# Cache pages laid out in 32 partitions with four tokens each, in place of 128 partitions with one

## The chip, the cores and the metric

One core of a Trainium2 chip runs the whole program in one launch. The metric is device microseconds from start to end, the median of the runs shown. All arithmetic is fp32, with matmul operands split into a high and a low part.

## The reference

One inference step of one decoder layer for two groups that share the weights: a prompt of 256 tokens, and 8 sample sequences of one new token each, whose past of 1024 tokens lies in paged caches (8 pages of 128 tokens for each sequence, found through `page_table`). The layer is: half a SwiGLU feed-forward, one input projection, two attention branches, an output projection, another half feed-forward.

For the samples, branch A (8 heads of 64) takes the scores of the new query against 1024 past keys, sums the keys in blocks of 256 tokens, keeps the three past blocks whose mean scores highest, adds ALiBi and does a softmax over these and the new token. Branch B (4 heads, two score maps of 64 each, values of 128) attends to all past tokens and subtracts lambda times the second softmax from the first. Each of the four caches (keys and values, A and B) holds rows of 512 numbers, 2 KB for each token, so a page is 256 KB in one piece of memory. All 8 sequences with 8 pages in four caches come to 256 pages, 64 MB.

What matters for the change: a softmax with ALiBi and block sums can take the tokens in any order, if the distance of each token and the block to which it belongs are known.

## The kernel before

The program is written out engine by engine, with semaphores between them; the order of each engine and of each DMA queue is the order in its block of code. The stages are: feed-forward 1, projection (w_in), the key stage (about 393 to 542 us), softmax beside the last two gate blocks (542 to 560 us), the value stage with the prompt's own attention (560 to 660 us), branch and output projections, feed-forward 2.

**Slots.** `kv` has two buffers for each of the branches A and B, and `kv_lent` one more, so `KVS` is 3. A buffer is [128, 4, 512], 8 KB in each partition, and holds half a sequence: four pages. One filling is called a use: uses 0 to 15 are keys, 16 to 31 are values, and each use brings 4 pages for A and 4 for B, 2 MB together. `load_half` (L380) issues four DMAs of one page; page q goes to column q of all 128 partitions, one token of 2 KB in each. A's are issued by SyncE, B's by GpSimd, from `kv_load`, which first waits until the use three before has been consumed, and for each new sequence reads 8 page numbers into registers (`page_ids`, L373). SyncE's queue also carries the 1 MB weight blocks (`load_w`, L448), one for each sequence in the key stage.

**Key stage.** `chunk_turn` (L1396) transposes for each chunk of 128 features the four pages' tokens into a PSUM bank, ScalarE (A, L716) and VectorE (B, L414) copy it to SBUF, and `chunk_scores` (L1405) multiplies by the padded query. Half a gate block (L1186 to L1188) stands behind each use of the first six sequences. The scores of all sequences and heads gather in two banks: partition = (head, sequence), column = token, 128 a page.

**Softmax.** VectorE reduces the scores to 4 block sums (L1036), ranks them (L1042 to L1048), adds page offset and penalty into 8 scalars (L1050), and writes `prob` = score + scalar + distance row for each page (L1052); ScalarE does the exponent; TensorE turns `prob` by a permutation (L1448).

**Value stage.** For each sequence and half, four matmuls with A's pages and four with B's (L1477): weights `wpad` (token = partition, page = column) against the page. Between them stand the prompt's scores, transposes and products. A slot comes free through `s_pv` when its four matmuls have ended, and `kv_load` then waits for it. After the last: the sample outputs are extracted (L1514) and the branch projections begin.

Of the kernel before, what the change touches and what calls it, by code (L numbers as in the profile page):

```python
# [19 lines left out]
ALU = mybir.AluOpType  # L20
ACT = mybir.ActivationFunctionType
AX = mybir.AxisListType

P = 128
# [9 lines left out]
PAST = 1024  # L34
# [8 lines left out]
KVS = 3  # L43
# [60 lines left out]
def _columns():  # L104
    at = 0
    for name, w in (("ident", 128), ("blockdiag", 128), ("ones", 128), ("half", 2), ("sel9", 9), ("sel8", 8), ("perm", 128), ("sel4", 4),
                    ("negslope", 1), ("pageslope", 8), ("coef1", 1), ("coeflam", 1), ("rowA", 1), ("tri", 16),
                    ("dist", 384), ("distrow", 128), ("maskA", 512), ("maskB", 512)):
        CW[name] = (at, w)
        at += w  # L110
    return at

NCONST = _columns()

def slope_of_row(j):

    return 2.0 ** -(j + 1) if j < 8 else 2.0 ** (-2.0 * ((j - 8) // 2 + 1))

def constants():
    c = np.zeros((P, NCONST), np.float32)

    def put(name, a):
        c[:, CW[name][0]:CW[name][0] + CW[name][1]] = a

    p = np.arange(P)
    put("ident", np.eye(P))
    put("blockdiag", p[:, None] // 64 == p[None] // 64)  # L130
    put("ones", 1.0)
    put("half", np.stack([p < 64, p >= 64], 1))
    put("sel9", (p[:, None] % 32) == np.arange(9)[None])

    row_s, row_j = p % 32 // 4, 8 * (p % 4 // 2) + 2 * (p // 32) + p % 2
    put("sel8", row_s[:, None] == np.arange(8)[None])

    put("perm", (64 * (row_j // 8) + 8 * row_s + row_j % 8)[:, None] == p[None])

    put("sel4", (p[:, None] % 32 // 8) == np.arange(4)[None])  # L140
    slope = np.array([slope_of_row(j) for j in row_j])
    put("negslope", -slope[:, None])
    put("pageslope", slope[:, None] * 128.0 * np.arange(8)[None])
    isb1 = (row_j >= 8) & (p % 2 == 1)
    put("coef1", (~isb1)[:, None])
    put("coeflam", isb1[:, None])
    put("rowA", (row_j < 8)[:, None])
    n = np.arange(4)
    put("tri", np.broadcast_to((n[None, :] < n[:, None]).reshape(1, 16), (P, 16)))
    k = np.arange(256)  # L150
    d0 = np.where(k[None, :128] <= p[:, None], p[:, None] - k[None, :128], BIG)
    d1 = np.where(k[None] <= p[:, None] + 128, p[:, None] + 128 - k[None], BIG)
    put("dist", np.concatenate([d0, d1], 1))
    put("distrow", np.broadcast_to(PAST - np.arange(128)[None], (P, 128)))
    col = np.arange(512)
    put("maskA", col[None] // 64 == p[:, None] % 8)
    put("maskB", col[None] // 128 == p[:, None] % 8 // 2)
    return c
# [26 lines left out]
def build(nc, A, O):  # L185
    ctx = ExitStack()
    with ctx:
# [3 lines left out]
        def place(name, shape, dt=F32, where=None):  # L191
            size = int(np.prod(shape[1:])) * 4
            where = where if where is not None else at
            h = nc.alloc_sbuf_tensor_at(name, shape, dt, offset=where[0])
            where[0] = (where[0] + size + 31) // 32 * 32
            assert where[0] <= end, (name, where[0], end)
            return h

        def sem(name):
            return ctx.enter_context(nc.semaphore(name))  # L200
# [7 lines left out]
        x = place("x", [P, KC, T])  # L208
# [15 lines left out]
        r = [region]  # L224
# [7 lines left out]
        r = [region]  # L232
# [5 lines left out]
        r = [region]  # L238
# [8 lines left out]
        stat = place("stat", [P, 64], where=r)  # L247
# [5 lines left out]
        r = [area]  # L253
# [4 lines left out]
        r = [area]  # L258
        kTs = [[place(f"kTs{a}{s}", [P, 512], where=r) for s in range(2)] for a in "AB"]
        r = [area]  # L260
        prob = place("prob", [P, PAST], where=r)
        b0 = place("b0", [P, P], where=r)
        ecur = place("ecur", [P, P], where=r)
        dcur = place("dcur", [TS, P], where=r)
        plog = [place(f"plog{h}", [P, 384], where=r) for h in range(2)]
        pts_at = r[0]
        r = [area]
        om = place("om", [P, 2, 512], where=r)
        r = [pts_at]
# [6 lines left out]
        r = [hlo_at]  # L276
        wpad = [place(f"wpad{s}", [P, NPG, 2, 56], where=r) for s in range(2)]

        bank = ctx.enter_context(nc.psum_tensor("bank", [P, 8, 512], F32))

        def C(name, lo=0, hi=None):
            a, w = CW[name]
            return const[:, a + lo:a + (w if hi is None else hi)]
# [22 lines left out]
        s_kv = [[sem(f"kv_landed{a}{s}") for s in range(KVS)] for a in "AB"]  # L306
# [59 lines left out]
        def kv_slot(ab, use):  # L366
            if use % KVS < KVS - 1:
                return kv[ab][use % KVS]
            return kv_lent[ab]

        def page_ids(eng, s):

            _, ids = nc.values_load_multi_w_load_instructions(A["page_table"][s:s + 1, 0:NPG], engines=[eng.engine], min_val=0, max_val=NPHYS - 1)  # L373
            return ids

        def load_half(eng, ab, cache, ids, half, use):

            for q in range(4):
                page = ids[4 * half + q]
                eng.dma_start(kv_slot(ab, use)[:, q, :], cache[bass.ds(page, 1)].rearrange("a t d -> (a t) d")).then_inc(s_kv[ab][use % KVS], 16)  # L380

        def kv_landed(use):
            return 64 * (use // KVS + 1)
# [3 lines left out]
        def kv_load(eng, ab, use):  # L387

            s, half = divmod(use % 16, 2)
            if half == 0:  # L390
                held[ab] = page_ids(eng, s)
            prev = use - KVS
            if use == KVS - 1:
                if ab == 0:
                    eng.wait_ge(s_lo, half_done(LENT_LAST, 1))
                else:
                    eng.wait_ge(s_ecur, 1)
            if 0 <= prev < 16:
                eng.wait_ge(s_kTs[ab], 4 * prev + 4)
            elif prev >= 16:  # L400
                eng.wait_ge(s_pv, 2 * (prev - 16) + ab + 1)
            load_half(eng, ab, (CACHE_K if use < 16 else CACHE_V)[ab], held[ab], half, use)
# [405 lines left out]
        def _(v):  # L808
            ch = Chain(v, s_vch)
            dve = nc.vector  # L810
# [222 lines left out]
            v.wait_ge(s_const_late, 16)  # L1033
            ch.link(dve.tensor_scalar(b0[:, :], C("distrow"), C("negslope"), None, ALU.mult))
            blk = stat[:, 8:12]
            ch.link(dve.tensor_reduce(blk, bank[:, 6:8, :].rearrange("p a (b n) -> p (a b) n", n=256), AX.X, ALU.add))  # L1036

            bm = blk.unsqueeze(1).broadcast_to([P, 4, 4])
            bn = blk.unsqueeze(2).broadcast_to([P, 4, 4])
# [6 lines left out]
            ch.link(dve.tensor_reduce(stat[:, 12:16], gt, AX.X, ALU.add))  # L1046
            ch.link(dve.tensor_scalar(stat[:, 12:16], stat[:, 12:16], 2.5, -BIG, ALU.is_gt, ALU.mult))
            ch.link(dve.tensor_scalar(stat[:, 12:16], stat[:, 12:16], C("rowA"), None, ALU.mult))  # L1048
            pen = stat[:, 12:16].unsqueeze(2).broadcast_to([P, 4, 2])
            ch.link(dve.tensor_tensor(stat[:, 48:56].rearrange("p (b g) -> p b g", b=4), C("pageslope").rearrange("p (b g) -> p b g", b=4), pen, ALU.add))  # L1050
            for g in range(NPG):
                ins = dve.scalar_tensor_tensor(out=prob[:, 128 * g:128 * g + 128], in0=bank[:, 6 + g // 4, 128 * (g % 4):128 * (g % 4) + 128],  # L1052
                                               scalar=stat[:, 48 + g:49 + g], in1=b0[:, :], op0=ALU.add, op1=ALU.add)
            ch.link(ins)
            ch.link(dve.tensor_reduce(stat[:, 2:3], prob[:, :], AX.X, ALU.max))
            ch.link(dve.tensor_tensor(stat[:, 2:3], stat[:, 2:3], ncur[:, :], ALU.max))
# [34 lines left out]
            for c in range(KC):  # L1091
                for h in range(2):
                    j = 2 * c + h
# [43 lines left out]
            for q in range(4):  # L1137
                ab, half = q // 2, q % 2
# [8 lines left out]
                g = gT[:, 8 * ab + 4 * half:8 * ab + 4 * half + 4, :]  # L1147
# [441 lines left out]
```

## Time and profile before

| what | value |
|---|---|
| median of 3 runs | 937.45 us (935.45 to 940.9) |
| profiled execution | 942.06 us, of which the span from first to last instruction is 940.4 |
| TensorE busy, weight loads busy | 834.4 us, 709.4 us |
| VectorE, ScalarE, GpSimd busy | 459.4, 359.0, 80.3 us |
| mean granted TensorE clock | 0.941 |
| moved by DMA | 209.73 MB, mean 223 GB/s |

TensorE is busy for 89% of the span, but the share is a mean over stages. The second part of the page cuts the span into 40 slices of 23.5 us; the digits are tenths. The chain of waits names what ended last at each moment. "DMA share" is the mean busy share of 16 DMA engines. `kvA` and `kvB` are the two own buffers of each branch, `kvA_lent` and `kvB_lent` the third.

### The profile page before, as it was taken

To read this page: it belongs to the slowest core of one execution; us is meant where nothing else is said; L and a number is where in the kernel's file an instruction comes from. 1 tells how busy PE (TensorE), PEld (TensorE's weight loads), DVE (VectorE), ACT (ScalarE), POOL (GpSimd) and SP (SyncE) were. 2 spreads that over 40 slices of the span, in tenths; PEclk is the share of its full clock that TensorE was granted. 3 is DMA by queue.
4 is the path that set the end of the run, shared out by engine and by line. 5 is a ranking of instruction groups with operands and counts; after the bars stand their busy time and mean duration, and the time that the engine had idled before them with its cause. 6 is when DMAs were issued, how large, how long until landed. Compare 5 with 4: busy or idle time off the path is not lost.

```text
span 940.4 us, 16984 instructions
## 1 busy us (share of the span) xinstructions
PE 834.4 (89%) x6366; PEld 709.4 (75%) x6366; DVE 459.4 (49%) x674; ACT 359.0 (38%) x539; POOL 80.3 (9%) x150
## 2 busy tenths in 40 slices
PE   3789999999997999689989896776989799999997
PEld 1369898989996989667767471321789699999997
DVE  1344444435436768634343364543475655555442
ACT  1344433343335454433233333321343544444341
POOL 0000000000001010222121213131000000000000
PEclk9789999999998999999999997787689799999999
DMA  8679898886766763578878858988045155555540
GB/s 317 239 253 307 275 310 267 295 294 196 257 230 233 249 205 106 181 246 276 282 244 287 311 176 298 345 318 308 1 135 179 48 181 181 180 191 172 178 147 24
DMA packets 146232, 209.73 MB, mean 223 GB/s; under 512 B 6693, under 2 KB 100148, under 8 KB 146172
## 3 DMA queue, kind: packets, MB, share of 16 engines
q1 hardware_dynamic: 134336, 170.97, 54.9%
q0 software_dynamic: 11360, 36.80, 11.0%
q10 hardware_dynamic: 476, 1.17, 0.3%
q8 instruction: 36, 0.59, 0.2%
q14 instruction: 24, 0.20, 0.1%
HBM read 205.67 MB, written 3.24 MB: 222 GB/s over the span
## 4 chain that ended last, share of the span: by engine, by line
PE 74%; DVE 7%; issue 6%; DMA 5%; ACT 4%; SPq 2%; POOLq 1%; POOL 0%; ACTq 0%; DVEq 0%
PE bank L1186 19%; PE bank L1187 18%; PE bank L1188 17%; PE bank L1396 6%; PE bank L1405 4%; PE bank L1213 4%; DVE rstd L967 2%; SPq L373 1%; ACT kTsA L716 1%; PE bank L1222 1%; DMA crow<-in_c_rows 1%; PE bank L1229 1%; DMA kvA_lent<-in_cache_v_moba 1%; PE bank L1477 1%; DMA raw<-in_w_ada 1%
## 5 line engine op out<-in xcount | busy, mean ns | idle before, releaser
L818 DVE TENSOR_TENSOR wlo<-raw,whi 128x1024 fp32r<-128x1024 f32 (+1 forms) x192 | 227.3, 1199 | 241.4 <-ACT whi L571 239.3
L1186 PE MATMUL bank<-hhi,whi 128*128 128x264 f32 x1088 | 321.8, 296 | 15.4 <-DVE hlo L858 12.9
L1187 PE MATMUL bank<-hlo,whi 128*128 128x264 f32 x1088 | 313.1, 288 | 0.0
L1188 PE MATMUL bank<-hhi,wlo 128*128 128x264 f32 x1088 | 312.5, 287 | 0.0
L571 ACT ACTIVATE whi<-raw 128x1024 fp32r<-128x1024 f32 (+1 forms) x192 | 194.8, 1036 | 134.2 <-PE bank L1188 79.5
L1186 PEld LDWEIGHTS bank<-hhi,whi 128*128 128x128 f32 x1088 | 209.1, 192 | 40.0 <-issue 29.5
L1187 PEld LDWEIGHTS bank<-hlo,whi 128*128 128x128 f32 x1088 | 210.2, 193 | 0.2
L1188 PEld LDWEIGHTS bank<-hhi,wlo 128*128 128x128 f32 x1088 | 208.8, 192 | 0.0
L1186 PE MATMUL bank<-ahi,whi 128*128 128x264 f32 x416 | 121.2, 291 | 4.0 <-DVE alo L1158 4.0
L1188 PE MATMUL bank<-ahi,wlo 128*128 128x264 f32 x416 | 119.2, 286 | 0.0
L1187 PE MATMUL bank<-alo,whi 128*128 128x264 f32 x416 | 119.1, 286 | 0.0
L1186 PEld LDWEIGHTS bank<-ahi,whi 128*128 128x128 f32 x416 | 79.5, 191 | 5.3 <-issue 5.0
L414 DVE COPY kTsB<-bank 128x512 f32<-128x512 f32 x64 | 41.8, 686 | 81.2 <-PE bank L1405 76.8
L1187 PEld LDWEIGHTS bank<-alo,whi 128*128 128x128 f32 x416 | 79.5, 191 | 0.2
L1188 PEld LDWEIGHTS bank<-ahi,wlo 128*128 128x128 f32 x416 | 79.6, 191 | 0.0
L716 ACT ACTIVATE kTsA<-bank 128x512 f32<-128x512 f32 x64 | 34.8, 595 | 86.6 <-PE bank L1405 81.5
L380 POOL DMA_DIRECT2D kvB<-in_cache_k_diff x44 | 23.6, 537 | 300.5 <-issue 235.7
L600 ACT ACTIVATE sil<-bank 128x528 f32<-128x528 f32 x22 | 13.4, 611 | 78.1 <-PE bank L1188 78.1
L1213 PE MATMUL bank<-raw,csilu 128*32 128x512 f32 x288 | 39.0, 660 | 2.4 <-DMA raw<-in_w_ada 2.1
L1396 PE MATMUL bank<-const,kvA 128*128 128x128 f32 x176 | 27.3, 279 | 13.2 <-ACT kTsA L716 13.2
L1396 PEld LDWEIGHTS bank<-const,kvA 128*128 128x128 f32 x176 | 20.3, 143 | 24.4 <-issue 21.1
L1405 PE MATMUL bank<-kTsA,qpad 128*32 128x512 f32 x128 | 34.7, 611 | 0.8 <-ACT kTsA L716 0.8
(215 smaller groups left out, 773.0 us busy)
## 6 DMA issues: line engine op xcount, KB each, us to landing
raw<-in_w_ada SPq DMA_DIRECT2D x36, 1024.0 KB, 7.4
raw<-in_ffn_w_gate SPq DMA_DIRECT2D x22, 1024.0 KB, 5.4
raw<-in_ffn_w_up SPq DMA_DIRECT2D x22, 1024.0 KB, 5.8
raw<-in_w_in SPq DMA_DIRECT2D x20, 1024.0 KB, 7.3
raw<-in_ffn_w_down SPq DMA_DIRECT2D x16, 1024.0 KB, 5.3
kvB<-in_cache_k_diff POOLq DMA_DIRECT2D x44, 256.0 KB, 5.8
kvA<-in_cache_k_moba SPq DMA_DIRECT2D x44, 256.0 KB, 4.1
kvA<-in_cache_v_moba SPq DMA_DIRECT2D x44, 256.0 KB, 5.9
```

The source lines that it names most:

```text
L380: eng.dma_start(kv_slot(ab, use)[:, q, :], cache[bass.ds(page, 1)].rearrange("a t d -> (a t) d")).then_inc(s_kv[ab][use % KVS], 16)
L414: copy(kTs[ab][g % 2][:, :], bank[:, 2 + 2 * (g % 2) + ab, :]).then_inc(s_kTs[ab], 1)
L571: nc.scalar.activation(half_view(whi[key[1] % 2], key, t), half_view(raw[s], key, t), ACT.Copy).then_inc(s_hi, 1)
L716: turned_chunk(a, 0, s, g, lambda out, in_: nc.scalar.activation(out, in_, ACT.Copy))
L818: dve.tensor_tensor(half_view(wlo[key[1] % 2], key, t), half_view(raw[s], key, t), half_view(whi[key[1] % 2], key, t).bitcast(F32), ALU.su ...
L967: dve.reciprocal(rstd[:, :, :], rstd[:, :, :]).then_inc(s_nvar, 1)
L1186: mm(out, wh, xh, start=start, stop=False)
L1187: mm(out, wh, xl, start=False, stop=False)
L1188: return mm(out, wl, xh, start=False, stop=stop)
L1213: ins = mm(bank[32 * j:32 * j + 32, 4, :], csilu[:, 4 * half + j, :], raw[s][:, 512 * j:512 * j + 512], start=(half == 0), stop=(half == 1))
L1396: ins = nc.tensor.transpose(bank[:, b, P * q:P * q + P], kv_slot(ab, use)[:, q, P * m:P * m + P], ident)
L1405: mm(bank[32 * m:32 * m + 32, 6 + g // 4, :], qpad[s % 2][:, 4 * ab + m, at_:at_ + 32], kTs[ab][g % 2][:, :], start=(s == 0 and g % 4 < 2) ...
```

## The change

`load_half` still issues four DMAs of one page each (256 KB). Page q now goes to the 32 partitions 32q to 32q+31, and fills the slot's whole 8 KB there: partition 32q+i gets tokens 4i to 4i+3 of page q, 8 KB in a row on both sides. Together the four pages fill the slot as before. The column index q of the slot, over which `chunk_turn` and the value matmuls run, is now the token modulo 4, and the partition tells page and token group. So a group of 128 score columns holds every fourth token of four pages; the instructions on TensorE stay the same in number and shape.

The softmax follows: the distance row depends on the column's partition of origin, `tokslope` (constants) takes the place of `pageslope`, the block sums are taken in two reductions (16 sums of 64 columns, then 4 of 4), and the penalty, which now differs inside a group of 128 columns, is added to the distance row in `bpen` (two rows of 128) instead of to the scalar. `bpen` takes 1 KB a partition behind `b0`.

```diff
--- before.py
+++ after.py
@@ -104,7 +104,7 @@
 def _columns():
     at = 0
     for name, w in (("ident", 128), ("blockdiag", 128), ("ones", 128), ("half", 2), ("sel9", 9), ("sel8", 8), ("perm", 128), ("sel4", 4),
-                    ("negslope", 1), ("pageslope", 8), ("coef1", 1), ("coeflam", 1), ("rowA", 1), ("tri", 16),
+                    ("negslope", 1), ("tokslope", 8), ("coef1", 1), ("coeflam", 1), ("rowA", 1), ("tri", 16),
                     ("dist", 384), ("distrow", 128), ("maskA", 512), ("maskB", 512)):
         CW[name] = (at, w)
         at += w
@@ -140,7 +140,9 @@
     put("sel4", (p[:, None] % 32 // 8) == np.arange(4)[None])
     slope = np.array([slope_of_row(j) for j in row_j])
     put("negslope", -slope[:, None])
-    put("pageslope", slope[:, None] * 128.0 * np.arange(8)[None])
+    g = np.arange(8)
+
+    put("tokslope", slope[:, None] * (512.0 * (g // 4) + g % 4)[None])
     isb1 = (row_j >= 8) & (p % 2 == 1)
     put("coef1", (~isb1)[:, None])
     put("coeflam", isb1[:, None])
@@ -151,7 +153,7 @@
     d0 = np.where(k[None, :128] <= p[:, None], p[:, None] - k[None, :128], BIG)
     d1 = np.where(k[None] <= p[:, None] + 128, p[:, None] + 128 - k[None], BIG)
     put("dist", np.concatenate([d0, d1], 1))
-    put("distrow", np.broadcast_to(PAST - np.arange(128)[None], (P, 128)))
+    put("distrow", np.broadcast_to(PAST - 128.0 * (p // 32) - 4.0 * (p % 32), (P, 128)))
     col = np.arange(512)
     put("maskA", col[None] // 64 == p[:, None] % 8)
     put("maskB", col[None] // 128 == p[:, None] % 8 // 2)
@@ -260,6 +262,7 @@
         r = [area]
         prob = place("prob", [P, PAST], where=r)
         b0 = place("b0", [P, P], where=r)
+        bpen = place("bpen", [P, 2, P], where=r)
         ecur = place("ecur", [P, P], where=r)
         dcur = place("dcur", [TS, P], where=r)
         plog = [place(f"plog{h}", [P, 384], where=r) for h in range(2)]
@@ -377,7 +380,7 @@
 
             for q in range(4):
                 page = ids[4 * half + q]
-                eng.dma_start(kv_slot(ab, use)[:, q, :], cache[bass.ds(page, 1)].rearrange("a t d -> (a t) d")).then_inc(s_kv[ab][use % KVS], 16)
+                eng.dma_start(kv_slot(ab, use)[32 * q:32 * q + 32, :, :], cache[bass.ds(page, 1)].rearrange("a (i j) d -> (a i) j d", j=4)).then_inc(s_kv[ab][use % KVS], 16)
 
         def kv_landed(use):
             return 64 * (use // KVS + 1)
@@ -1033,7 +1036,8 @@
             v.wait_ge(s_const_late, 16)
             ch.link(dve.tensor_scalar(b0[:, :], C("distrow"), C("negslope"), None, ALU.mult))
             blk = stat[:, 8:12]
-            ch.link(dve.tensor_reduce(blk, bank[:, 6:8, :].rearrange("p a (b n) -> p (a b) n", n=256), AX.X, ALU.add))
+            ch.link(dve.tensor_reduce(stat[:, 32:48], bank[:, 6:8, :].rearrange("p a (b n) -> p (a b) n", n=64), AX.X, ALU.add))
+            ch.link(dve.tensor_reduce(blk, stat[:, 32:48].rearrange("p (a j x) -> p a x j", a=2, x=2), AX.X, ALU.add))
 
             bm = blk.unsqueeze(1).broadcast_to([P, 4, 4])
             bn = blk.unsqueeze(2).broadcast_to([P, 4, 4])
@@ -1046,11 +1050,12 @@
             ch.link(dve.tensor_reduce(stat[:, 12:16], gt, AX.X, ALU.add))
             ch.link(dve.tensor_scalar(stat[:, 12:16], stat[:, 12:16], 2.5, -BIG, ALU.is_gt, ALU.mult))
             ch.link(dve.tensor_scalar(stat[:, 12:16], stat[:, 12:16], C("rowA"), None, ALU.mult))
-            pen = stat[:, 12:16].unsqueeze(2).broadcast_to([P, 4, 2])
-            ch.link(dve.tensor_tensor(stat[:, 48:56].rearrange("p (b g) -> p b g", b=4), C("pageslope").rearrange("p (b g) -> p b g", b=4), pen, ALU.add))
+            pen = stat[:, 12:16].unsqueeze(2).broadcast_to([P, 4, 64]).rearrange("p (a x) n -> p a x n", a=2)
+            base = b0[:, :].rearrange("p (x n) -> p x n", x=2).unsqueeze(1).broadcast_to([P, 2, 2, 64])
+            ch.link(dve.tensor_tensor(bpen[:, :, :].rearrange("p a (x n) -> p a x n", x=2), base, pen, ALU.add))
             for g in range(NPG):
                 ins = dve.scalar_tensor_tensor(out=prob[:, 128 * g:128 * g + 128], in0=bank[:, 6 + g // 4, 128 * (g % 4):128 * (g % 4) + 128],
-                                               scalar=stat[:, 48 + g:49 + g], in1=b0[:, :], op0=ALU.add, op1=ALU.add)
+                                               scalar=C("tokslope", g, g + 1), in1=bpen[:, g // 4, :], op0=ALU.add, op1=ALU.add)
             ch.link(ins)
             ch.link(dve.tensor_reduce(stat[:, 2:3], prob[:, :], AX.X, ALU.max))
             ch.link(dve.tensor_tensor(stat[:, 2:3], stat[:, 2:3], ncur[:, :], ALU.max))
```

## Rows read from the trace of the kernel before

**Rows 1.** The page's 40 equal slices of the span: granted clock, DMA share.

```profile
PEclk9789999999998999999999997787689799999999
DMA  8679898886766763578878858988045155555540
```

**Rows 2.** Busy time by stretch; columns: start:end, length, engines, then clock, DMA share, GB/s.

```profile
404.40:534.00 129.60, 116.72 (x958) 87.80 (x956) 53.13 (x82) 47.13 (x76) 30.09 (x56) 1.00 0.79 270
545.00:559.00 14.00, 13.15 (x109) 12.27 (x107) 10.06 (x33) 3.63 (x7) 1.81 (x4) 1.00 0.47 151
559.00:660.00 101.00, 70.38 (x419) 25.72 (x420) 42.56 (x122) 28.87 (x98) 27.98 (x52) 0.79 0.86 302
585.00:610.00 25.00, 18.48 (x106) 7.81 (x106) 12.05 (x33) 8.62 (x26) 6.57 (x13) 0.77 0.99 348
```

**Rows 3.** The chain of waits in the key stage: start us, length us, what.

```profile
419.57 1.75 PE bank L1396 x16
421.32 1.07 PE bank L1405 x7
422.39 0.60 ACT kTsA L716
...
429.18 0.87 PE bank L1396 x8
...
534.04 1.94 PE bank L1396 x16
```

**Rows 4.** SyncE's queue in order of time: start us, length us, instruction.

```profile
404.44 11.50 SPq L380 DMA_DIRECT2D kvA<-in_cache_k_moba  x8
...
528.73 1.88 SPq L380 DMA_DIRECT2D kvA<-in_cache_v_moba  x4
```

**Rows 5.** Line 1477, the value matmuls: idle time of TensorE before them, by releaser (us, times).

```profile
  DMA kvA<-in_cache_v_moba: 20.8, 8
  DMA kvA_lent<-in_cache_v_moba: 20.2, 6
...
  DMA kvB<-in_cache_v_diff: 14.3, 8
```

**Rows 6.** The chain of waits in the value stage.

```profile
560.95 0.33 SPq L380
...
574.33 3.96 SPq L373
...
586.36 10.33 DMA kvA_lent<-in_cache_v_moba
...
645.35 8.80 DMA kvB<-in_cache_v_diff
```

**Rows 7.** DMA queues and issues, 559 to 660 us; issues: KB each, median us to landing.

```profile
q1 hardware_dynamic: 10096, 16.78, 48.7%
q0 software_dynamic: 4160, 13.63, 36.7%
...
kvA<-in_cache_v_moba SPq DMA_DIRECT2D x36, 256.0 KB, 5.9
kvB<-in_cache_v_diff POOLq DMA_DIRECT2D x36, 256.0 KB, 6.7
```

**Rows 8.** VectorE's groups from 541 to 560 us: busy us, mean ns.

```profile
L1036 DVE TENSOR_REDUCE stat<-bank 128x4 f32<-128x1024 f32 x1 | 1.2, 1225 | 0.0
...
L1034 DVE TENSOR_SCALAR b<-const 128x128 f32<-128x128 f32 x1 | 0.3, 287 | 1.2 <-PE bank L1405 1.2
...
L1050 DVE TENSOR_TENSOR stat<-const,stat 128x8 f32<-128x8 f32 x1 | 0.2, 168 | 0.0
```

**Rows 9.** VectorE in order of time, then the chain of waits, at the softmax.

```profile
552.45 0.75 DVE L1062 TENSOR_SCALAR prob<-prob,stat 128x1024 f32<-128x1024 f32 x1
...
555.86 2.00 PE bank L1448 x16
```

## The prediction

> **What bounds the kernel now.** I started from the 40 slices [rows 1]. Counted from 0, the DMA engines are busy for seven tenths or more from slice 17 to 27, while the page transfers run, but for slice 23 with the softmax; and the granted clock, 0.9 or more in nearly all slices before, falls to 0.7 and 0.8 in slices 24 to 27, the value stage: TensorE waits there. Then the stretches [rows 2]: key stage 270 GB/s at a DMA share of 0.79 and a clock of 1.00, softmax 151 GB/s, value stage 302 GB/s at 0.86, with 25 us at 348 GB/s and 0.99. So there are two regimes.
>
> In the key stage the chain of waits [rows 3] is TensorE's own work: transposes, scores, one ScalarE copy, and half a gate block, again and again, 9.6 us for each use (419.57 to 429.18). No step of it is a DMA. In the value stage the idle time before the value matmuls is 20.8 + 20.2 + 14.3 us [rows 5], all of it ended by a page's landing, and the chain there [rows 6] goes slot freed, page numbers read (3.96 us), DMA issued, 10.33 us to landing, and at the end 8.80 us for the last B page. This stretch is bound by how fast pages come in, nothing else.
>
> The profiled execution took 942.06 us, 1.7 more than its span, and 4.6 more than the median of 937.45. I work in the span and apply the difference to the median.
>
> **What the change does, part by part.**
>
> *Bytes and issues.* Unchanged: 256 pages of 256 KB, four DMAs for each use and branch, by the same queues behind the same waits. A use brings 2.10 MB (eight pages).
>
> *Pieces.* A page is now 32 runs of 8 KB in place of 128 of 2 KB. What a piece costs beside its bytes can be bounded by the two queues [rows 7]: SyncE's moved 16.78 MB in 48.7% of 16 engines' 101 us, which is 21.3 GB/s for an engine while it is busy; GpSimd's, whose packets are larger (13.63 MB in 4160, against 16.78 in 10096), 23.0 GB/s. If 8 KB pieces bring A to B's rate, A's half of a use is 8% cheaper, the whole use 4%. At 351 GB/s (302 over 0.86) a use takes 6.0 us, so this is 0.24 us for each, and 13 uses are loaded inside the value stage (19 to 31): 3 us. Fewer pieces may also shorten the time to landing (5.9 and 6.7 us, [rows 7]), which stands on the chain a handful of times; at most some 1 us each, 5 in all. Bounds of this part: 0 and -8 us; at an unchanged rate I would take -5.
>
> *Place.* Before, every page transfer, as every weight transfer, spreads over all 128 partitions; after, each lies in a quarter, in the order 0 to 31, 32 to 63, and so on, and both queues walk through the quarters in the same order. If the way into SBUF is divided among the partitions, a page can reach only part of it. The trace of before has no large transfer that covers less than 128 partitions, so this must be bounded. Upper end: the 351 GB/s of now, if the way in is not divided, or if different pages in flight fill each other's gaps. Lower end: half, 176 GB/s, if the pages in flight mostly stand in one half. (A quarter would need both queues in the same quarter all the time; I give it no share.) I take 260, the middle: two queues run at once, and they are in different halves some of the time, since B's issue starts later than A's and its waits are other ones.
>
> The Trainium skill ("SBUF — State Buffer", section "Door 1: The DMA port swizzle") speaks directly against this change: it says that partitions 0 to 31, or 0 to 63, reach just 8 of the 16 DMA ports, and gives 189 GB/s against 328 for 1 MB transfers. Its ratio of 0.58 would make 202 GB/s of our 351, an estimate from that page; no run here has shown it yet. The same page says that two DMAs at once, one in each half, gained only 6%, which would leave little of the mixing on which my 260 rests.
>
> What 260 GB/s costs. Key stage: a use takes 2.10 MB / 260 = 8.1 us, and seven weight blocks of 1.05 MB at 351 take 3.0 each. SyncE issues use 3 at 404.44 [rows 4] and TensorE comes to use 15, the last, at 534.04 [rows 3]: 129.6 us for 13 uses and seven blocks, 13 x 8.1 + 21 = 126. It just fits, behind TensorE, at a price of 0. Three value uses are then loaded beside the softmax, where the DMA share is now 0.47 [rows 2]; 3 x 8.1 = 24 us from 528.73 on [rows 4], done before 560. Value stage: from the first refill at 560.95 to the last landing at 645.35 + 8.80 = 654.15 [rows 6] there are 93 us for 13 uses (27.3 MB) and one weight block. At 351 GB/s that is 78 + 3 = 81, so 12 us are gaps (page numbers, first landing). After: 105 + 3, and of the gaps I keep 5, since slower transfers overlap them: 113 us. **+20 us.** With the gaps gone or whole it is +15 to +27.
>
> *VectorE.* The added reduction over 16 sums is some 170 ns, like the 168 ns of another short step (L1050); the one over PSUM keeps its 1024 elements (L1036, 1225 ns), the penalty add grows from 8 columns (168 ns) to 256; by the 287 ns of 128 columns it is some 415 ns [rows 8]. Together 0.2 + 0.25 = +0.45 us with its semaphore step. The cover is the last gate block: VectorE ends `prob` at 552.45 + 0.75 = 553.2, and TensorE comes to the permutation at 555.86 [rows 9], 2.7 us later. So 0; without the cover +0.45.
>
> *TensorE.* Same instructions. Longer waits in the value stage keep its clock down, but it waits there already. 0.
>
> Sum: 937.45 + 20 = 957.5; 958.
>
> **Rivals.**
>
> *A: the rate stays.* For it: the engines are 0.99 busy at 348 GB/s [rows 2], which could be their own limit and not that of the way in, and eight pages may be queued at once, so that quarters mix. Against: both queues take the quarters in one order. Price: 0 to -8 us from the pieces, most likely -5: 932.5. The change decides for faster only if the rate of pages stays above about 27.3 MB / (93 - 3 - 5 us) = 321 GB/s; below this each use comes later.
>
> *B: the two queues stand in the same half nearly always.* For it: their issues in the key stage follow the same chunks, so A and B start within a microsecond or two. At 218 GB/s (62% of now) a use takes 9.6 us. Key stage: 13 x 9.6 + 21 = 146 against 129.6, so that transfers become its bound too, +16. Value stage: 125 + 3 + 3 = 131 against 93, +38. Sum +54: 991. At 176 GB/s the same sums give 176 - 130 = +46 and 158 - 93 = +65, 1048.
>
> *C: the pieces are not joined* and a page still goes as 128 runs of 2 KB. Then the gain of part one is 0 and the loss by place stands; it changes A's price to 0, "no change".
>
> **How the numbers follow.** Forecast (220 to 320 GB/s): 0.40. B (under 220): 0.20. A: 0.38, of which 0.25 gains more than half a per cent (4.7 us, about what a measurement can tell) and 0.13 stays within it, C included. The last 0.02 are losses of another kind. Faster 0.25, same 0.13, slower 0.62. The forecast's own range is 943 to 980. The range for 8 in 10 must take in most of A, down to 930, and the first half of B, up to 1000.
>
> **What would show it.** If right: DMA share near 1 and GB/s near 260 through the value stage; the landings of pages grow from 6 us towards 10; more idle before L1477, ended by DMA; key stage still 9.6 us a use, on TensorE, with no DMA on its chain; and L1448 still starts right behind the gates. The first sign for B is a key stage longer than 9.6 us a use, with DMA waits before L1396. For A: 350 GB/s or more at 585 to 610 us with less idle before L1477. The forecast is wrong if the rate of pages is above 320 or under 220 GB/s, or if the time before 404 or behind the value stage moves by more than 3 us.

## The result, and the profile after

The changed kernel takes 1001.75 us (median of 4 runs, 990.44 to 1007.98) against 938.24, which is 63.5 us more; the ratio is 1.064, 95% interval 1.056 to 1.072, or 60 us. (Ratios and intervals leave out executions that count as disturbed: one of these four, the 1007.98, without which the median is 998.33, three of the four of experiment 2, which so has no ratio, and one of the six of experiment 12.) The profiled execution has a span of 1003.5 us against 940.4. The direction held, the size did not: 20 us were forecast, 60 to 63.5 measured. The time lies at the upper end of the stated range (1000), by the median of all four just above it, and near that of rival B (991 at 218 GB/s).

The slices of the changed kernel, granted clock, DMA share and GB/s:

```profile
PEclk9999999999999999998979797767679899999999
DMA  8678889875679736899999959999814346555541
GB/s 309 234 259 295 295 272 301 298 239 190 234 233 251 226 129 193 201 248 224 240 222 225 221 138 233 235 228 252 222 45 140 110 133 197 173 176 189 180 136 33
```

The GB/s of the kernel before:

```profile
GB/s 317 239 253 307 275 310 267 295 294 196 257 230 233 249 205 106 181 246 276 282 244 287 311 176 298 345 318 308 1 135 179 48 181 181 180 191 172 178 147 24
```

From slice 17 to 27, counted from 0, the DMA engines are now at nine tenths or more, but for slice 23 with the softmax, and still move only 221 to 252 GB/s, where they moved 244 to 345 at a share of seven to nine tenths [rows 1]. The engines are busier and carry less. Two stretches (key stage to the last key page's landing, value stage; columns as in [rows 2]):

```profile
404.40:567.30 162.90, 123.31 (x969) 91.82 (x965) 54.93 (x83) 48.72 (x78) 29.36 (x60) 0.92 1.00 226
...
594.90:720.00 125.10, 68.35 (x409) 24.06 (x413) 41.62 (x119) 28.04 (x95) 25.48 (x52) 0.73 1.01 234
```

The value stage moves 234 GB/s at a share of 1.01, where it had 302 at 0.86 [rows 2], and takes from 594.9 to its last landing at 719.3. (The share is worked out from the packets' times and can pass 1 by a little.) The clock falls from 0.79 to 0.73, and in the key stage from 1.00 to 0.92, in both with TensorE waiting.

The key stage was TensorE's [rows 3]. The chain of waits of the changed kernel there:

```profile
431.40 1.75 PE bank L1401 x16
...
441.00 1.75 PE bank L1401 x16
...
447.75 19.82 DMA kvA<-in_cache_k_moba
...
494.81 22.59 DMA kvA_lent<-in_cache_k_moba
...
541.97 25.27 DMA kvA<-in_cache_k_moba
```

A use whose pages are there still takes 9.6 us (431.40 to 441.00), but now and then a page is not there: three landings of 19.82, 22.59 and 25.27 us stand on the chain. Line 1401 (1396 before) now has idle time that a DMA ends, of which there was none:

```profile
  DMA kvA<-in_cache_k_moba: 44.6, 7
...
  DMA kvA_lent<-in_cache_k_moba: 20.7, 3
```

What waits before the value matmuls (L1482, before [rows 5]: 20.8 + 20.2 + 14.3 and a rest of 1.2):

```profile
  DMA kvA<-in_cache_v_moba: 52.9, 12
  DMA kvB<-in_cache_v_diff: 26.7, 14
  DMA kvA_lent<-in_cache_v_moba: 23.4, 6
...
  DMA kvB_lent<-in_cache_v_diff: 9.9, 5
```

That is 112.9 us against 56.5, in which TensorE waits for a page. The chain of waits in the value stage (before [rows 6]):

```profile
609.41 16.39 DMA kvA<-in_cache_v_moba
...
629.50 37.65 DMA kvA<-in_cache_v_moba
...
699.54 19.74 DMA kvB<-in_cache_v_diff
```

Landings of 16 to 38 us stand there, where the two of before had 10.33 and 8.80. And the queues from 594 to 720 us (before [rows 7]):

```profile
q1 hardware_dynamic: 3816, 15.49, 53.0%
q0 software_dynamic: 2496, 13.63, 46.5%
...
kvA<-in_cache_v_moba SPq DMA_DIRECT2D x36, 256.0 KB, 16.2
kvB<-in_cache_v_diff POOLq DMA_DIRECT2D x36, 256.0 KB, 15.5
```

While it is busy with SyncE's queue, each engine moves 15.49 MB / (0.530 x 16 x 126 us) = 14.5 GB/s, where it moved 21.3; with GpSimd's queue it is also 14.5, against 23.0. The median landing goes from 5.9 and 6.7 us to 16.2 and 15.5.

Where the 63 us of the span went, by the start of the value matmuls and the last landing: 559.7 became 594.9 (+35.2, key stage and what it delays), and 654.15 became 719.3 (another +29.9, value stage). Outside these two stages the differences are some 2 us each way: the same step of TensorE starts at 412.20 us and not at 409.98 (part of the 35.2), and what follows the last landing is 2.0 us shorter.

### The profile page after: what moved, and what is told of

The parts are those of the page before. It is cut to its first block, busy times and chain, and to the rows that moved or that the text cites. A ratio compares the mean times of both kernels' runs of the same rounds, so it can differ in the third digit from the quotient of the medians.

```text
span 1003.5 us, 16985 instructions
## 1 busy us (share of the span) xinstructions
PE 843.3 (84%) x6366; PEld 713.0 (71%) x6366; DVE 459.8 (46%) x675; ACT 358.8 (36%) x539; POOL 74.2 (7%) x150
## 3 DMA queue, kind: packets, MB, share of 16 engines
q1 hardware_dynamic: 122048, 170.97, 57.8%
q0 software_dynamic: 7264, 36.80, 15.6%
## 4 chain that ended last, share of the span: by engine, by line
PE 64%; DMA 19%; DVE 6%; issue 4%; ACT 3%; SPq 2%; POOLq 0%; POOL 0%; ACTq 0%; DVEq 0%
PE bank L1191 17%; PE bank L1192 16%; PE bank L1193 16%; DMA kvA<-in_cache_v_moba 5%; DMA kvA<-in_cache_k_moba 4%; PE bank L1401 4%; DMA kvB<-in_cache_v_diff 4%; PE bank L1218 3%; PE bank L1410 2%; DMA kvA_lent<-in_cache_k_moba 2%; DVE rstd L970 2%; SPq L383 2%; PE bank L1227 1%; DMA crow<-in_c_rows 1%; DMA raw<-in_ffn_w_up 1%
## 5 line engine op out<-in xcount | busy, mean ns | idle before, releaser
L1401 PE MATMUL bank<-const,kvA 128*128 128x128 f32 x176 | 29.7, 296 | 31.7 <-DMA kvA<-in_cache_k_moba 20.1
L1482 PE MATMUL bank<-kvA,wpad 128*32 128x512 f32 x88 | 15.7, 795 | 30.7 <-DMA kvA<-in_cache_v_moba 29.2
L1084 DVE SCALAR_TENSOR_TENSOR plog<-const,bank 128x384 f32<-128x384 f32 x16 | 8.8, 551 | 69.7 <-PE bank L1447 69.7
```

Source lines behind the costliest of these rows:

```text
L1401: ins = nc.tensor.transpose(bank[:, b, P * q:P * q + P], kv_slot(ab, use)[:, q, P * m:P * m + P], ident)
```

## The experiments

**1. Small pieces in the same 32 partitions.**

```diff
-    kv_slot(ab, use)[32 * q:32 * q + 32, :, :], ... .rearrange("a (i j) d -> (a i) j d", j=4)
+    kv_slot(ab, use)[32 * q:32 * q + 32, :, :], ... .rearrange("a (j i) d -> (a i) j d", j=4)
```

(the line is shortened; `tokslope` and `distrow` are changed to match)

> The changed kernel, but partition 32q+i takes tokens i, 32+i, 64+i, 96+i of page q, so that each page still lies in 32 partitions but goes as 128 pieces of 2 KB (distances adapted, output unchanged). Theory 'place' (a transfer that covers 32 partitions reaches only part of the way into SBUF, whatever its pieces): as slow as the changed kernel, 1000 us within 8, value stage near 235 GB/s. Rival 'pieces' (8 KB pieces are slow by themselves; the median packet would be the cause and not the sufferer): back near 938 us, 300 GB/s or more.

Measured: 1007.94 us, ratio 1.073 (1.065 to 1.081). Its value stage:

```profile
593.00:718.00 125.00, 73.09 (x397) 26.85 (x397) 41.93 (x121) 28.67 (x97) 28.76 (x52) 0.70 1.02 235
```

This is the rate of the changed kernel. The size of the pieces is not what costs: 2 KB pieces in 32 partitions are as slow as 8 KB ones. In the trace, the median time of a 2 KB packet is 146 ns here and 84 ns in the value stage of before.

**2. Pages issued in the order 0, 2, 1, 3.**

```diff
-            for q in range(4):
+            for q in (0, 2, 1, 3):
```

> The changed kernel with one edit: the four pages of a use are issued in the order 0, 2, 1, 3 in place of 0, 1, 2, 3, so that consecutive pages of one queue lie in partitions 0-31, 64-95, 32-63, 96-127. Theory 'halves' (partitions 0 to 63 share one half of the ways in, 64 to 127 the other): the engines' transfers mix the halves sooner, pages at 260 to 330 GB/s, 945 to 980 us. Rival 'each transfer by itself' (a page transfer is slow whatever stands beside it in the queue): no change, 1000 us. Rival 'pieces': 1000 us.

Measured: 992.03 us, 974.36 to 994.67 in four runs, too uneven for a ratio. Inconclusive on how much this order regains, but it does not repair the layout. Experiment 12 takes it up.

**3. The two queues in opposite halves.**

```diff
-            for q in range(4):
+            for q in ((0, 1, 2, 3), (2, 3, 0, 1))[ab]:
```

> The changed kernel with one edit: B's queue issues its pages in the order 2, 3, 0, 1, A's stays 0, 1, 2, 3, so that the two queues start in different halves of the partitions. Theory 'halves': A and B start within 2 us in the key stage, so both halves are in use at once; 945 to 975 us, a larger part regained in the key stage than in the value stage. Rival 'each transfer by itself' and rival 'pieces': 1000 us.

Measured: 1004.11 us, ratio 1.071 (1.065 to 1.077). A miss for my theory of mixing: nothing is regained in all. In the profiled execution the value matmuls do start at 585.6 us, 9 us before those of the changed kernel, but the value stage moves less than with equal order (215 for 234 GB/s) and gives that back.

```profile
404.40:534.00 129.60, 106.48 (x840) 81.85 (x839) 46.06 (x69) 40.77 (x65) 23.50 (x48) 0.93 1.02 227
586.00:721.00 135.00, 75.61 (x409) 27.76 (x405) 41.47 (x118) 28.00 (x93) 25.63 (x52) 0.68 1.01 215
```

**4. Every fourth partition.**

```diff
-    kv_slot(ab, use)[32 * q:32 * q + 32, :, :]
+    kv_slot(ab, use)[q:P:4, :, :]
```

(the distances, block sums and penalties are changed to match)

> The changed kernel with page q in partitions q, q+4, q+8, ... (32 partitions that span all 128), still 8 KB pieces; the block sums and penalties are adapted, output unchanged. Theory 'place by range' (what counts is how much of the 128 partitions a transfer spans): full rate, 925 to 945 us. Rival 'pieces': 1000 us. A third outcome, if the 16 engines take two neighbouring partitions each and pairs of engines still meet on the same way in: no gain over the changed kernel, 990 to 1005 us.

Measured: 941.99 us, ratio 1.0005 (0.9964 to 1.0045). Key and value stage:

```profile
404.40:534.00 129.60, 116.87 (x960) 87.96 (x958) 53.21 (x81) 47.26 (x77) 28.97 (x56) 1.00 0.78 270
559.00:660.00 101.00, 71.99 (x417) 26.79 (x417) 42.36 (x121) 29.09 (x99) 26.90 (x52) 0.75 0.80 298
```

The whole loss is gone, with 32 partitions for each page as before the edit, the same 8 KB pieces, read from the same places in memory, and the same order of pages. So it is which 32 partitions. The run also measures the pieces alone, at the full rate: they bring nothing that shows. The queues of its value stage:

```profile
q1 hardware_dynamic: 4655, 16.34, 43.5%
q0 software_dynamic: 2496, 13.63, 36.1%
...
kvA<-in_cache_v_moba SPq DMA_DIRECT2D x36, 256.0 KB, 6.0
```

SyncE's queue is at 16.34 MB / (0.435 x 16 x 101 us) = 23.2 GB/s for a busy engine, GpSimd's at 23.4: the gain of an engine's time that I had derived is there. The packets say the same: the median of an 8 KB one is 309 ns, and four of 2 KB at 84 are 336. The gain does not come out in the time. The engines are busy for 0.80 of the stage only, and a page of A lands 6.0 us after its issue, before 5.9; that this is the reason is argued, not shown.

**5. The disputed cost by itself.** Pages are loaded in twelve sections, with nothing beside them. Where each section's page i goes (a summary, not the code):

```text
all128: buf[:, i, 0:512]                quarter0: buf[0:32, i, :]
quarters01 / 02 / 0123: buf[32*k:32*k+32, i, :], k in turn
step4: buf[i%4::4, i, :]                evenlow: buf[0:64:2, i, :]
two_...: 8 pages from SyncE, 8 from GpSimd
```

> Measures the disputed cost by itself: no step of the layer is computed, only pages are loaded, 16 pages (4.2 MB) in each of twelve sections with nothing beside them, each section waited out; seven sections from SyncE's queue alone, five with 8 pages from SyncE's and 8 from GpSimd's queue. Rival 'a quarter is a quarter of the ways': quarter 0 near 100 GB/s, quarters 0 and 1 in turn near 200. Rival 'span' (a transfer is served by the share of 128 partitions that it spans): quarter 0 near 100, every second partition of 0 to 63 near 200.

Measured in one execution, one stretch inside each section, in the order just given, then the five with two queues (both all 128; both quarter 0; quarter 0 and quarter 2; both all four in turn; both every fourth). The last two columns are DMA share and GB/s:

```profile
4.00:12.00 8.00, 0.00 (x0) 0.00 (x0) 1.00 0.99 357
20.00:34.00 14.00, 0.00 (x0) 0.00 (x0) 1.00 1.02 203
42.00:57.00 15.00, 0.00 (x0) 0.00 (x0) 1.00 1.03 205
65.00:78.00 13.00, 0.00 (x0) 0.00 (x0) 1.00 1.02 228
86.00:99.00 13.00, 0.00 (x0) 0.00 (x0) 1.00 1.02 218
106.00:113.00 7.00, 0.00 (x0) 0.00 (x0) 1.00 0.97 343
121.00:136.00 15.00, 0.00 (x0) 0.00 (x0) 1.00 1.02 202
143.00:150.00 7.00, 0.00 (x0) 0.59 (x2) 1.00 1.01 366
158.00:173.00 15.00, 0.00 (x0) 0.00 (x0) 1.00 1.02 203
180.00:192.00 12.00, 0.00 (x0) 0.00 (x0) 1.00 1.02 245
200.00:214.00 14.00, 0.00 (x0) 0.00 (x0) 1.00 1.02 221
221.00:227.00 6.00, 0.00 (x0) 0.01 (x1) 1.00 0.90 362
```

All 128 partitions: 357 GB/s. Quarter 0: 203. Quarters 0 and 1 in turn: 205, no better, so these two share their ways ("ways" here are paths into the partitions, known only by such rates). Quarters 0 and 2 in turn: 228. All four in turn, the layout of the change: 218. Every fourth partition: 343. Every second of the lower 64: 202. A quarter of the partitions is thus not a quarter of the ways (rival one, 100 GB/s), nor does span count (rival two: every second of 64 would beat quarter 0). One quarter gets a little over half of the full rate (203 of 357). Two queues in opposite halves reach 245, 20% more than two in the same quarter (203) and far from 366.

In every slow section the share is 1.02 or 1.03: the engines count as busy while they are held up, the median 8 KB packet taking 645 ns in quarter 0 and 309 ns in every fourth partition. A full DMA share is here no sign that the engines are the limit.

The Trainium skill ("SBUF — State Buffer", "Door 1: The DMA port swizzle") states a rule for this: bit 6 of the partition number chooses the half, bits 4 to 2 one of eight ports in it, bit 5 nothing. The sections agree on bits 6 and 5; that bits 4 to 2 choose a port, no section tests. Its measured 189 GB/s for 32 partitions, from 1 MB transfers, is near the 4.2 MB / 22.7 us = 185 GB/s of the whole section of quarter 0, first issue and last landing included. For two DMAs at once, one in each half, the Trainium skill ("SBUF — State Buffer", "Can I just issue two DMAs to hit both halves?") gives 6% over one alone. Here it is 20% (245 against the 203 of one queue), which is more, but still far from twice the rate.

**6. The VectorE part alone.**

```diff
-    kv_slot(ab, use)[32 * q:32 * q + 32, :, :], ... .rearrange("a (i j) d -> (a i) j d", j=4)
+    kv_slot(ab, use)[:, q, :], ... .rearrange("a t d -> (a t) d")
```

(the line is shortened; what this kernel leaves out is the match of distances and tokens)

> The changed kernel with the load of before (each page over all 128 partitions) and the changed VectorE steps; the distances then belong to other tokens than those loaded, the work is the same. The prediction's step: the added 0.45 us hide behind the last gate block, 0 change: ratio 1.000 within 0.4%. Rival (the cover is gone, or the longer block sums cost more): +0.5 to +1.5 us, up to 1.0016, which this run could not tell from 0; a ratio above 1.005 would refute the step.

Measured: 939.5 us, ratio 1.0022 (0.9992 to 1.0053). No change that can be told from zero. In the changed kernel's own trace, VectorE's last step on `prob`:

```profile
588.12 0.75 DVE L1067 TENSOR_SCALAR prob<-prob,stat 128x1024 f32<-128x1024 f32 x1
```

and TensorE's next step on the chain:

```profile
591.05 2.00 PE bank L1453 x16
```

`prob` ends at 588.87, 2.2 us ahead of the permutation; before it was 2.7.

**7. Keys alone.**

```diff
+                if use >= 16:
+                    ... (the load of before)
+                    continue
```

> The changed kernel with quarters for the key pages alone; the value pages lie over all 128 partitions as before, so values are weighted with the wrong tokens' weights, the work is the same. If the two stages add up as the traces show (start of the value matmuls 35 us later, its last landing another 30): +33 to +38 us, 971 to 978. Rival 'one backlog' (slow keys delay the values' first loads, and slow values alone would explain most of the loss): +10 to +20 us.

Measured: 962.66 us, ratio 1.027 (1.022 to 1.033), some 26 us: less than the 33 to 38 I expected, and more than the rival's 10 to 20. The value matmuls start at 585.9 and not at 594.9. The first value pages are issued from 546 us on, beside the last keys, and wide value pages could explain the 9 us. This is not shown: experiment 3, with its values in quarters, starts at 585.6 as well.

**8. The page numbers read earlier.** The kernel before, with the next sequence's numbers read before the odd use's wait:

```diff
-            if half == 0:
+            if use == 0:
                 held[ab] = page_ids(eng, s)
+            ids = held[ab]
+            if half == 1 and use < 4 * TS - 1:
+                held[ab] = page_ids(eng, (use + 1) % 16 // 2)
```

> A version that the traces point to: the kernel before with the page numbers of the next sequence read into registers before the wait of the odd use, in place of after it. The read takes 4 to 8 us of each queue and stands on the chain in the value stage. Theory 'the read is exposed': 2 to 10 us faster, 928 to 936. Rival 'moved, not hidden' (the odd use's issue is late by the same time, since its slot is free already): no change within 3 us.

Measured: 932.42 us, ratio 0.9928 (0.9897 to 0.9959), 7 us faster. The value stage:

```profile
557.00:650.00 93.00, 64.12 (x417) 25.47 (x417) 42.10 (x121) 28.64 (x98) 27.96 (x52) 0.83 0.91 326
```

It moves 326 GB/s in 93 us, where before it was 302 in 101. So when the numbers are read matters, by 7 us. The 3.96 us of [rows 6] are only the first load of one read, which lasts from 574.33 to 582.02; six such reads lie in the stage on each queue. On the chain of before from 559 to 655 us the reads (L373) have 13.5% on SyncE's queue and 9.4% on GpSimd's, more than the 20.0% of the two landings. They do not leave the chain here: from 557 to 648 us SyncE's have 24.2%, and GpSimd's none.

**9. Wide transfers beside quarters.** Loads only, in one execution: 8 pages over all 128 partitions from SyncE, 8 from GpSimd.

> Loads pages only, as the first measurement of this kind, no step of the layer. Why did the key stage lose so much, although 7 MB of its transfers are weights over all 128 partitions? Theory 'held up': each engine takes turns between the two queues, so a wide transfer beside quarters waits behind the slow pieces and the sum stays near 220 to 250 GB/s (a 2 KB piece of 84 ns and an 8 KB piece of 645 ns make 16 x 10.2 KB in 729 ns, 225 GB/s) for wide beside the four quarters in turn and wide beside quarter 0. Rival 'only the pages are slow': wide pieces fill the unused ways, the sum is 300 GB/s or more. Wide beside every fourth partition and wide beside wide: 340 or more. Every second partition of 64 to 127, one queue: 200 to 205, like the lower half. Every third partition from 0 (0 to 93): a test of whether span or halves count; two of three rows lie in the lower half, so between 203 and 343, I take 270.

Measured, wide beside the four quarters in turn; beside quarter 0; beside every fourth; beside wide; then alone every second partition of 64 to 127; every third of 0 to 93:

```profile
19.00:26.00 7.00, 0.00 (x0) 0.32 (x1) 1.00 1.06 240
37.00:44.00 7.00, 0.00 (x0) 0.56 (x2) 1.00 1.04 238
55.00:63.00 8.00, 0.00 (x0) 0.84 (x2) 1.00 1.01 374
68.00:76.00 8.00, 0.00 (x0) 1.54 (x3) 1.00 1.03 382
84.00:97.00 13.00, 0.00 (x0) 0.00 (x0) 1.00 1.02 203
105.00:115.00 10.00, 0.00 (x0) 0.00 (x0) 1.00 0.96 266
```

A wide transfer beside quarters brings the sum to 240 GB/s, not to 370: it is held up with them. In that stretch (19 to 26 us) SyncE's queue, the wide one, moved 0.57 MB and GpSimd's 1.11 MB. So the key stage's weight blocks do not go at 351 GB/s, as I had taken. The sum was forecast, the way to it was not right: I had left a wide 2 KB piece at 84 ns and let it wait its turn, but the median 2 KB packet itself takes 153 ns beside the quarters, and 84 beside every fourth partition. The rest fell where expected: 203 for the upper half, 266 for every third.

**10. Values alone**, the mirror of 7 (`if use < 16` in its edit).

> The changed kernel with quarters for the value pages alone, the key pages over all 128 partitions as before (keys are then scored at the wrong distances, the work is the same). Keys alone cost 25 us of the 63.5. Theory 'they add up': +38 us, within 6. Rival 'backlog' (the keys' delay overlaps the values' first loads, so that each alone costs less than its share or more): +28 us or less, or +48 or more.

Measured: 973.88 us, ratio 1.035 (1.027 to 1.042), 33 us. The key stage is at its old 270 GB/s, the value stage at the 234 of the changed kernel:

```profile
404.00:534.00 130.00, 117.09 (x962) 88.25 (x961) 53.65 (x81) 47.17 (x76) 29.95 (x56) 1.00 0.82 270
562.00:686.00 124.00, 74.59 (x385) 26.84 (x381) 40.05 (x112) 26.74 (x87) 25.01 (x51) 0.65 1.03 234
```

With 26 for the keys that is 59 of the 60 us that the ratio of the whole change makes: the parts add up.

**11. Every fourth partition and the early read.** The edits of 4 and 8 together.

> Every fourth partition with 8 KB pieces, and the page numbers read ahead; output unchanged. The early read alone gave a ratio of 0.993. Theory 'cheaper pieces pay once the read is out of the way': 0.985 to 0.990, 924 to 929 us. Rival 'the pieces bring nothing here' (the engines are not the bound between the peaks): the same 0.993.

Measured: 933.27 us, ratio 0.9917 (0.9892 to 0.9941). Its interval covers that of 8, so the larger pieces bring nothing here either. This and 8 are the versions that beat both kernels; 8 is the simpler.

**12. Both orders combined.**

```diff
-            for q in range(4):
+            for q in ((0, 2, 1, 3), (2, 0, 3, 1))[ab]:
```

> The changed kernel with both orders combined: A's queue issues its pages 0, 2, 1, 3, B's 2, 0, 3, 1, so that neighbours in a queue lie in different halves and the two queues start in different halves: the best mixing that order alone can give. The separate measurement gave 245 GB/s for two queues in opposite halves, 228 for one queue that alternates, against 218 for the order of the change. Theory 'mixing is worth at most 20%': pages at 230 to 250 GB/s, 980 to 998 us. Rival 'mixing was only spoilt by the order in the two runs before': 300 GB/s or more, 940 to 960 us.

Measured: 989.44 us, ratio 1.053 (1.048 to 1.058). Key and value stage:

```profile
404.40:534.00 129.60, 109.94 (x874) 84.23 (x872) 48.58 (x74) 43.16 (x68) 25.58 (x52) 0.95 1.02 237
577.00:700.00 123.00, 76.48 (x397) 27.04 (x389) 40.07 (x112) 26.70 (x87) 25.64 (x52) 0.68 1.02 248
```

That is 237 and 248 GB/s, for 227 and 215 in experiment 3. The two orders together regain some 10 of the 60 us (1.053 for 1.064, though the two intervals overlap by a little); the rival's 300 GB/s is out.

## Why the prediction was right or wrong

**What bounds the kernel now: right in the main.** The key stage was on TensorE and the value stage on how fast pages come in. Slower pages hit the second in full and the first only once they no longer fit behind TensorE. "Nothing else" was too strong: the reads of page numbers stood on the chain for about as long as the landings (8).

**Place: the mechanism was right, the term mis-sized, and this is the first of the two steps that failed.** I bounded the page rate by 176 and 351 GB/s and took 260, about the middle, on the ground that two queues are in different halves some of the time. Measured alone, the layout gives 218 to 221 GB/s (5), and with the program's weights 226 and 234. The ground did not hold: even two queues kept in opposite halves reach only 245 by themselves (5), and in the program the order of pages gains nothing (3) or some 10 us (12). My own sum at 218 gave +54. That this 218 lies so near the measured rate is partly luck, since no row of the trace of before gave it.

**The key stage's overlap: wrong, the second step that failed.** "It just fits, at a price of 0" rested on the 260, and on seven weight blocks at 351 GB/s, 3.0 us each. But wide transfers are held up beside quarters (9), and the landings in the key stage grow. The changed kernel from 404 to 577 us, KB and median us to landing:

```profile
kvA<-in_cache_k_moba SPq DMA_DIRECT2D x36, 256.0 KB, 11.3
...
raw<-in_w_in SPq DMA_DIRECT2D x4, 1024.0 KB, 24.7
```

and the kernel before, 412 to 508 us, where a page of A had 4.4:

```profile
raw<-in_w_in SPq DMA_DIRECT2D x4, 1024.0 KB, 9.8
```

So what was to hide behind TensorE became the bound. My 13 uses and seven blocks are 34.6 MB, 153 us at the measured 226 GB/s against the 129.6 us at hand. To the landing of the last key page it took 162.9 us (226 x 162.9 = 36.8 MB), since value pages were by then under way beside it. That is +33 where the sum had 0. With the weights left at 351 GB/s my way of adding up would have given only 13 x 9.3 + 21 = 142 us, +12, even at the measured rate; so the rate alone does not explain this stage. In the value stage I forecast 113 us for 93, and it is 719.3 - 596.1 = 123 from the first refill at 596.14: +30 where the sum had +20.

**Pieces: the engine's time right, its worth wrong.** At an unchanged rate I took -5 us, a ratio of 0.995; measured is 1.0005 (0.9964 to 1.0045) in experiment 4. Rival A's gain was not there even without its obstacle.

**VectorE: right.** Its part is 0 within 0.5% (6), and `prob` is still ready 2.2 us ahead of the permutation.

**Rivals.** B had 0.20 and is nearest to what happened (226 and 234 GB/s, where it said under 220), though by another way: not because the queues start together (3 and 12 undid that) but because opposite halves help little. C is refuted: SyncE's queue has 122048 packets for the 134336 of before, 96 fewer for each of its 128 pages, as 32 runs in place of 128 make; GpSimd's has 7264 for 11360, 32 fewer. And unjoined pieces would have changed nothing (1).
## What to carry to other kernels

Transfers into 32 neighbouring partitions got 0.57 of the rate of those over 128 (203 against 357 GB/s), and so did 32 partitions spread over one half, 0 to 63 or 64 to 127; one transfer over 64 neighbouring partitions was not measured. They also slow the wide transfers beside them (240 GB/s in sum). If only 32 partitions are to be written by a DMA, take every fourth (343). Larger pieces brought nothing here, though an engine's time fell by 8%; look at the GB/s beside the DMA share, since a held-up engine counts as busy too. And when a rate is known only by two far bounds and is put in the middle because "they mix some of the time", do not take the mixing for granted: measure it alone first, as experiment 5 does, or give the unmixed case the larger chance.

## What was not expected of the hardware

Two queues in opposite halves reach 245 GB/s, where the two halves' 203 each would allow 366, the rate of two wide queues. A wide transfer is slowed packet by packet beside quarters: the median 2 KB packet goes from 84 to 153 ns. And a piece of 8 KB costs an engine little less than four of 2 KB: a busy engine moves 23.2 GB/s against 21.3, in the value stage of experiment 4 and of the kernel before.
